# Two feed-forward blocks: the residual, the norm and the first gate/up tiles worked by halves of the tokens

## What is computed

```python
def rms_norm(x, g):
    xf = x.astype(jnp.float32)
    y = xf * lax.rsqrt(jnp.mean(xf * xf, axis=-1, keepdims=True) + RMS_EPS)
    return (y * g.astype(jnp.float32)).astype(x.dtype)

def conv_ffn(h, w_up, conv_w, conv_b, w_down):
    u = h @ w_up
    up = jnp.pad(u, ((0, 0), (CONV_W - 1, 0), (0, 0)))
    y = conv_b
    for j in range(CONV_W):
        y = y + up[:, j:j + S] * conv_w[j]
    gate, val = jnp.split(y, 2, axis=-1)
    return (jax.nn.silu(gate) * val) @ w_down
...
        x = x + g1 * mix
        h = rms_norm(x, norm_ffn[i]) * (1.0 + sc2) + sh2
        x = x + g2 * conv_ffn(h, ffn_w_up[i], ffn_conv_w[i], ffn_conv_b[i], ffn_w_down[i])
```

## Time and profile before

| | us |
|---|---|
| median of 3 runs | 1971.48 |
| lowest and highest | 1970.94, 1976.03 |
| profiled execution, its own time | 1970.52 |
| span from its first to its last instruction | 1968.7 |
| PE busy of the span | 1924.3 |

### The profile page before, as it was taken

The page is one execution under the profiler, slowest core; times in us unless marked ns, Lnnn a source line. Parts: engine busy times, 40 slices in busy tenths (PEclk is TensorE's granted clock), DMA queues, the critical chain, the costliest instruction groups (busy, mean ns, idle before and its releaser), DMA issues.

```text
span 1968.7 us, 26692 instructions
## 1 busy us (share of the span) xinstructions
PE 1924.3 (98%) x9254; PEld 1548.9 (79%) x9254; DVE 1084.2 (55%) x1657; ACT 562.4 (29%) x1119; POOL 1245.7 (63%) x729
## 2 busy tenths in 40 slices
PE   9999999999999899998999999999989999999999
PEld 7867788888888777777888888877766778888887
DVE  5966498877778325463443442144988543434412
ACT  4135300001124335661311121133457431111210
POOL 7642688887667565564766666645775357666664
PEclk9999999999999899999999999989999999999999
DMA  7520377766543222114332333213210023233331
GB/s 276 212 78 23 107 258 254 246 234 206 195 143 92 69 75 65 44 43 150 97 96 96 96 96 96 96 55 96 86 65 1 22 65 117 96 96 96 97 96 64
DMA packets 62326, 221.15 MB, mean 112 GB/s; under 512 B 6907, under 2 KB 7163, under 8 KB 62124
## 3 DMA queue, kind: packets, MB, share of 16 engines
q1 hardware_dynamic: 45216, 161.71, 25.7%
q10 hardware_dynamic: 17036, 58.46, 8.1%
HBM read 218.00 MB, written 2.14 MB: 112 GB/s over the span
## 4 chain that ended last, share of the span: by engine, by line
PE 92%; DVE 3%; POOL 2%; issue 2%; ACT 1%; DMA 0%; SPq 0%; POOLq 0%; DVEq 0%; ACTq 0%
PE bank L310 26%; PE bank L312 25%; PE bank L311 25%; PE bank L966 2%; PE bank L799 2%; PE bank L345 2%; PE bank L350 1%; PE bank L346 1%; PE bank L458 1%; PE bank L925 1%; PE bank L976 1%; PE bank L821 1%; POOL w_lo L1310 1%; PE bank L603 1%; PE bank L808 1%
## 5 line engine op out<-in xcount | busy, mean ns | idle before, releaser
L1310 POOL TENSOR_TENSOR w_lo<-raw,w_hi 128x1024 fp32r<-128x1024 f32 (+1 forms) x304 | 765.3, 2518 | 24.9
L310 PE MATMUL bank<-a_hi,w_hi 128*128 128x512 f32 x1960 | 764.7, 390 | 0.7 <-POOL w_lo L1310 0.4
L312 PE MATMUL bank<-a_hi,w_lo 128*128 128x512 f32 x1960 | 762.8, 389 | 0.0
L311 PE MATMUL bank<-a_lo,w_hi 128*128 128x512 f32 x1960 | 762.6, 389 | 0.0
L1305 POOL TENSOR_SCALAR w_hi<-raw 128x1024 fp32r<-128x1024 f32 x298 | 344.3, 1155 | 469.5 <-PE bank L312 360.4
L310 PEld LDWEIGHTS bank<-a_hi,w_hi 128*128 128x128 f32 x1960 | 367.9, 188 | 77.3 <-POOL w_lo L1310 0.8
L312 PEld LDWEIGHTS bank<-a_hi,w_lo 128*128 128x128 f32 x1960 | 367.9, 188 | 76.7
L311 PEld LDWEIGHTS bank<-a_lo,w_hi 128*128 128x128 f32 x1960 | 368.0, 188 | 76.1
L1904 DVE SCALAR_TENSOR_TENSOR tmp<-bank,vecs,tmp 128x511 f32<-128x511 f32 x88 | 65.9, 749 | 263.5 <-ACT tmp L1595 263.5
L1889 DVE CUSTOM_DVE_ANT_0 y<-y,cond 128x1024 f32<-128x1024 f32 x84 | 197.7, 2387 | 0.0
L1595 ACT ACTIVATE tmp<-bank,vecs 128x512 f32<-128x512 f32 x88 | 68.5, 781 | 372.7 <-PE bank L312 364.9
(11 more groups left out here) (295 smaller groups left out, 2250.5 us busy)
## 6 DMA issues: line engine op xcount, KB each, us to landing
raw<-in_stream SPq DMA_DIRECT2D x299, 512.0 KB, 3.5
y<-in_ada ACTq DMA_DIRECT2D x96, 512.0 KB, 4.6
x<-in_x SPq DMA_DIRECT2D x4, 512.0 KB, 6.5
bias<-in_bias ACTq DMA_DIRECT2D x1, 2048.0 KB, 14.8
y<-rel_rows ACTq DMA_DIRECT2D x1, 2048.0 KB, 8.1
bias<-rel_rows ACTq DMA_DIRECT2D x1, 2048.0 KB, 15.0
out<-x SPq DMA_DIRECT2D x8, 256.0 KB, 2.0
cond<-in_c ACTq DMA_DIRECT2D x1, 512.0 KB, 7.7
```

Source lines behind the costliest of these rows:

```text
L310: pe.matmul(o, lhs_hi, rhs_hi, start=start, stop=False, **kw)
L311: pe.matmul(o, lhs_hi, rhs_lo, start=False, stop=False, **kw)
L312: return pe.matmul(o, lhs_lo, rhs_hi, start=False, stop=stop, **kw)
L1310: m = pool.tensor_tensor(w_lo[:, s, part], raw[:, j, part], f32(w_hi[:, s, part]), ALU.subtract)
```

## The change

In both joints the last four output tiles and the first four gate/up tiles are worked in two halves of 256 tokens, h=0 and h=1.

- PE makes output tiles 0 to 3 as before, then tiles 4 to 7 for the tokens of h=0, then tiles 4 to 7 for those of h=1, with matmuls of 256 columns (`pe_late_halves`). Two tiles share a bank: tiles 4 and 5 of h=0 lie in bank 0, 6 and 7 in bank 1, those of h=1 in banks 2 and 3. The sum of squares of h=0 is taken after tile 4 of h=1, its spread after tile 5 of h=1.
- The gate/up tiles 0 to 3 follow in this order (`pe_early_halves`): tiles 0, 1 of h=0; the sum of squares of h=1; tiles 2, 3 of h=0 for five chunks; the spread of h=1; the last three chunks; then h=1 with all four tiles for chunks 0 and 1, tiles 0 and 1 for chunks 2 to 7, tiles 2 and 3 for chunks 2 to 7.
- `x`, the squares and their sum move in 12 pieces, 4 whole chunks and 2 x 4 halves; the running sum lies in `bank[7]` and no longer in SBUF. The scaled chunk lies in `bank[4]` or `bank[6]` (256 columns), no longer in `tmp`.
- DVE makes every low part, 16 halves. POOL makes none, and ACT's second copy goes. POOL's queue then holds only splits there.
- A block of output weights 4 to 7 is finished only with its tile of h=1, so POOL begins on gate/up blocks 0 to 3 at that point. `INVERSE_LAT` and `INVERSE_Q` only renumber counters of the inverse roots.

```diff
+HALVED = ("ffn0", "ffn1")
+HALF = S // 2
+HALF_PIECES = 4 + 2 * 4
+EARLY_SHARED = 2
...
+        def late_tile(c, h):
+
+            return bank[2 * h + (c - 4) // 2][:, HALF * (c % 2):HALF * (c % 2) + HALF]
...
+        def pe_late_halves(pe, name, norm):
+
+            for h in range(2):
+                for c in range(4, DC):
+                    s = (START[name] + c) % SPLIT
+                    if h == 0:
+                        pe.wait_ge(split_ready, START[name] + 1 + c)
+                    if c % 2 == 0:
+
+                        pe.wait_ge(x_ready, X_AT[name] + 2 * h + (c - 4) // 2 + 1)
+                    for k in range(DC):
+                        m = pe_three_passes(pe, late_tile(c, h), w_hi[:, s, k * P:(k + 1) * P], w_lo[:, s, k * P:(k + 1) * P],
+                                            a_hi[:, k, tokens_of(h)], a_lo[:, k, tokens_of(h)], k == 0, k == DC - 1, skip_group_check=True)
+                    m.then_inc(block_done if h else half_done, 1)
+                    if h and c == 4:
+                        pe_sum_half(pe, norm, 0)
+                    if h and c == 5:
+                        pe_spread_half(pe, norm, 0)
...
+            pe.wait_ge(split_ready, START[name] + 2)
+            products(0, (0, 1), range(DC))
+            pe_sum_half(pe, norm, 1)
+            pe.wait_ge(split_ready, START[name] + 4)
+
+            pe.wait_ge(x_ready, X_AT[update] + HALF_PIECES)
+            products(0, (2, 3), range(5))
+            pe_spread_half(pe, norm, 1)
+            products(0, (2, 3), range(5, DC))
+
+            products(1, range(4), range(EARLY_SHARED))
+            products(1, (0, 1), range(EARLY_SHARED, DC))
+            products(1, (2, 3), range(EARLY_SHARED, DC))
...
+            for c in range(DC):
+                scale(0, c)
+                if c:
+                    low(0, c - 1)
+                if c in (1, 2):
+                    add_piece(7 + c)
+                if c == 4:
+                    late_tiles(6, 1)
+                if c in (5, 6):
+                    add_piece(5 + c)
+            low(0, DC - 1)
+            inverse(1)
+            v.wait_ge(rstd_ready, NORM_INDEX[name] + 2)
+            for c in range(DC):
+                scale(1, c)
+                if c:
+                    low(1, c - 1)
+            low(1, DC - 1)
...
-            split_stream(START["out2"] + SPLIT + 2, START["gu2"] + AHEAD)
-            pool_lows("ffn0")
-            split_stream(START["gu2"] + AHEAD, START["qi"] + AHEAD)
+            split_stream(START["out2"] + SPLIT + 2, START["qi"] + AHEAD)
...
-            pe_tiles(pe, "out2", "battn", norm="ffn0")
-            pe_norm(pe, "ffn0", 1)
-            pe_tiles(pe, "gu2", "ffn0")
+            pe_tiles(pe, "out2", "battn", end=4)
+            pe_late_halves(pe, "out2", "ffn0")
+            pe_early_halves(pe, "gu2", "ffn0", "out2")
+            pe_tiles(pe, "gu2", done=4)
```

More of the change, by code:

```diff
@@ L354, in pe_tile_pair, with tokens_of, piece, pe_sum_half @@
                     after(k)
-        def pe_tiles(pe, name, split=None, norm=None):
-            n = COUNT[name]
+        def tokens_of(h):
+            return slice(HALF * h, HALF * h + HALF)
+        def piece(p):
+            if p < 4:
+                return p, slice(0, S)
+            return 4 + p % 4, tokens_of(p // 4 - 1)
+        def late_tile(c, h):
+            return bank[2 * h + (c - 4) // 2][:, HALF * (c % 2):HALF * (c % 2) + HALF]
+        def pe_sum_half(pe, name, h):
+            pe.wait_ge(sq_added, ADDED_AT[name] + (7, HALF_PIECES - 1)[h])
+            if h:
+                pe.wait_ge(scaled_ready, T_AT[name] + DC)
+            for t in (2 * h, 2 * h + 1):
+                m = pe.matmul(sum_columns(name)[:, t:t + 1], square_sum[:, GROUP_AT[name] % 2, t * P:(t + 1) * P], ones[:, 0:1],
+                              start=t == 2 * h, stop=True, skip_group_check=True)
+            m.then_inc(group_used, 1)
@@ new lines, in pe_early_halves, with products @@
+        def pe_early_halves(pe, name, norm, update):
+            pe_begin(pe, name)
+            pe.wait_ge(x_ready, X_AT[update] + 8)
+            def products(h, tiles, chunks):
+                sets = [(j, bank[j][:, tokens_of(h)], (START[name] + j) % SPLIT) for j in tiles]
+                for k in chunks:
+                    cols = slice(k * P, (k + 1) * P)
+                    pe.wait_ge(hi_ready, SPLIT_AT[norm] + DC * h + k + 1)
+                    for _, o, s in sets:
+                        pe.matmul(o, w_hi[:, s, cols], a_hi[:, k, tokens_of(h)], start=k == 0, stop=False, skip_group_check=True)
+                        pe.matmul(o, w_lo[:, s, cols], a_hi[:, k, tokens_of(h)], start=False, stop=False, skip_group_check=True)
+                    pe.wait_ge(lo_ready, LOW_AT[norm] + DC * h + k + 1)
+                    for _, o, s in sets:
+                        m = pe.matmul(o, w_hi[:, s, cols], a_lo[:, k, tokens_of(h)], start=False, stop=k == DC - 1, skip_group_check=True)
+                        if h and k == DC - 1:
+                            m.then_inc(block_done, 1)
+            pe.wait_ge(split_ready, START[name] + 2)
[9 more added lines that the diff above has]
+            products(1, (2, 3), range(EARLY_SHARED, DC))
@@ L360, in pe_tiles @@
+        def pe_tiles(pe, name, split=None, norm=None, done=0, end=None):
+            n = COUNT[name] if end is None else end
             follows = {"u": "z", "q": "u"}.get(name)
-            if not follows and name not in ("ki", "pe_gate"):
+            if not follows and name not in ("ki", "pe_gate") and not done:
                 pe_begin(pe, name)
-            done = 0
             if split == "attn":
@@ L445, in sum_columns @@
         def sum_columns(name):
+            if name in HALVED:
+                return rstd_bank[:, HALF:HALF + TT]
             return (bank[0] if name in ("post_ffn", "mix1") else bank[4])[:, 0:TT]
@@ L1559, in _ @@
                          lambda c: low_done("dattn", c), ready=((q_placed, 14), (q_placed_late, 2)))
-            pe_tiles(pe, "out3", "dattn", norm="ffn1")
-            pe_norm(pe, "ffn1", 1)
-            pe_tiles(pe, "gu3", "ffn1")
+            pe_tiles(pe, "out3", "dattn", end=4)
+            pe_late_halves(pe, "out3", "ffn1")
+            pe_early_halves(pe, "gu3", "ffn1", "out3")
+            pe_tiles(pe, "gu3", done=4)
             pe_down(pe, "down3", 2)
@@ L1918, in dve_conv, with dve_residual @@
             turn(FC // 2 - 1, split=True)
-        def dve_residual(v, update, layer, which, ready, n, norm=None):
-            slow = n == 4
+        def dve_residual(v, update, layer, which, ready, norm=None):
             for c in range(DC):
-                if norm and c and slow:
-                    dve_add_square(v, norm, c - 1)
                 ready(c)
-                v.scalar_tensor_tensor(x[:, c, :], bank[c % n][:], mod(layer, which, c), x[:, c, :], ALU.mult,
+                v.scalar_tensor_tensor(x[:, c, :], bank[c][:], mod(layer, which, c), x[:, c, :], ALU.mult,
                                        ALU.add).then_inc(x_ready, 1)
-                if norm and c and not slow:
+                if norm and c:
                     dve_add_square(v, norm, c - 1)
```

154 lines of the change are left out of this document (120 added, 34 removed).

## The result

The changed kernel takes 1959.07 us (median of 4 runs, 1957.28 to 1960.39) beside 1971.82 us for the kernel before on the same chip, 12.7 us less. The ratio of their runs is worked out apart and is not the quotient of the two medians: 0.9927 with a 95% interval of 0.9913 to 0.9942, which stands for 14.4 us less (11.4 to 17.2). Two later comparisons gave 0.9932 (0.9918 to 0.9946) and 0.9928 (0.9915 to 0.9942). The profiled execution took 1960.39 us, with a span of 1958.6 us.

What follows compares the result with a forecast made beforehand. PE, busy for 98% of the span, was taken as the bound. A stretch of 45.3 + 2.0 + 0.3 = 47.6 us, against 54.2 and 53.4, gains 12.4 us together, giving 1959.1 us; range 1955.5 to 1966.5.

Steps and rivals of the forecast that it cites:

- 384 half matmuls: Output tiles 4 to 7 and gate/up tiles 0 to 3 in halves: 45.3 us of PE time a stretch.
- four insertions: Two half sums and two half spreads between PE's matmuls in each stretch: 0.5 us each, together 2.0 us.
- waits: PE's waits for other engines in each block's stretch: nothing waits, but 0.3 us put in for thin slacks.
- The pitch: Time for a 256-column matmul on PE in the stretches: 0.118 us, with bounds 0.1133 and 0.120.
- The clock: PE at the joints: without long standstills the granted clock no longer falls; in block 2 the fall cost 2.5 us.
- The loss of the joint goes whole: Block 2's joint: PE's 7.11 us of only sums and transposes, 2.5 of fallen clock and 0.9 of sum all go.
- DVE keeps up: Block 2's stretch: DVE's 22 operations at some 0.45 us end at 934.4, 0.8 us before PE asks.
- The rival with 0.6 us: DVE becomes the bound in both stretches, at 0.6 us for an operation: 1967.5 us; chance 0.15.
- POOL keeps up: Gate/up tiles 2 and 3 of h=0: POOL's four splits, 3.53 us each, end 1.1 us before PE asks.
- The weight load: Rival: 188 ns weight loads no longer hidden under PE's 256-column matmuls, each stretch 26.9 us longer, 2013 us; chance 0.07.

Runs made afterwards that it cites:

- all-halved kernel: The kernel before, with gate/up tiles 4 to 43 of blocks 2 and 3 made of 256-column matmuls: 1997.34 us beside 1974.78, ratio 1.0125.
- the kernel with the norm behind the tiles: The changed kernel, with sum and spread of h=0 behind output tile 7 of h=1 in both blocks: 1969.62 us beside 1974.78, ratio 0.998.
- held up alone: The kernel before, with unread matmuls in PE's three waits at both joints: 1971.35 us beside 1974.78, ratio 0.9986.
- the experiment: The changed kernel, with six more 256-column DVE operations ahead of the first scaling of h=0 in blocks 2 and 3: ratio to the kernel before 0.9945.

## Why the prediction was right

Forecast 1959.1 us, measured 1959.07; forecast gain 12.4, stretches 12.97. That the two times agree to 0.03 us is luck: the changed kernel's own medians were 1959.07, 1960.21 and 1957.25. The closeness of the stretch, too, owes something to terms that cancel, so here they are one by one:

| term | predicted | measured |
|---|---|---|
| 384 half matmuls | 45.3 (0.118 each) | 46.1 (0.120) |
| four insertions | 2.0 | 1.3 |
| waits | 0.3 | 0.0 |
| sum | 47.6 | 47.35 |

- **The pitch** was mis-sized by 0.002 us. The full stream shows 0.120, the upper of the two figures taken from the earlier trace rows. But those rows don't hold it: starts printed to 0.01 us give a pair's half distance no closer than to 0.005, and the 32 pairs together lie at 0.118 as read. So the attention's matmuls, with one weight tile again and again, do start 0.002 us closer than these, and 0.120 as a bound came out by the rounding of one row. In the all-halved kernel the same weights twice in a row made no difference, so what makes the 0.002 us stays open.
- **The insertions** were put too high. A half sum was right (0.45 for 0.5). A half spread was put at 0.5 us, from the whole one's 1.11 us at the fallen clock, and took 0.21: a price read at 1.2 GHz doesn't hold where the clock stays up, and a row's length holds the draining too (the half spread's row is 0.38 us long here, with the next start 0.13 us behind its own).
- **The clock.** That it would not fall was right, PEclk 1.00 in both stretches. That its fall had cost 2.5 and 1.3 us was right for the kernel before as a part of a sum, and not as a price: held up alone it gave 1.24 and 0.47, since POOL's split of gate/up tile 2 stood 0.8 us behind it.
- **The loss of the joint goes whole**, 7.11 + 2.5 + 0.9: right, and shown by the kernel with the norm behind the tiles, which gives 5.7 of it back a joint.
- **DVE keeps up.** 22 operations were put at 0.45 us and an end at 934.4, 28.4 us into the stretch; the last low part of h=0 ended at 936.98, also 28.4 us in. Its slack, put at 0.8, is 0.8 by the trace and 0.55 by the experiment. The groups by line show why no operation was long:

```profile
L2105 DVE SCALAR_TENSOR_TENSOR a_lo<-bank,mods,a_hi 128x256 fp32r<-128x256 f32 x32 | 15.4, 480 | 1.2 <-ACT a_hi L1250 1.2
L2100 DVE SCALAR_TENSOR_TENSOR bank<-x,gains,bank 128x256 f32<-128x256 f32 x32 | 15.2, 485 | 6.1 <-PE bank L392 5.6
L2080 DVE SCALAR_TENSOR_TENSOR x<-bank,mods,x 128x256 f32<-128x256 f32 x16 | 7.0, 480 | 19.5 <-PE bank L322 19.5
L2077 DVE TENSOR_TENSOR bank<-bank,squares 128x256 f32<-128x256 f32 x12 | 5.1, 428 | 0.6
```

  0.48 us as put, from the row of another line. The rival with 0.6 us did not come. The rule that speaks against small tiles (the Trainium skill, VectorE: DVE Perf Modes, "The TRN2 errata — SBUF-src ops pay a fixed extra latency per instruction") holds in its cost: 480 ns for 256 columns against the 750 of the earlier trace rows for 512 leaves 210 ns that don't shrink, and DVE's busy time rose by 4 us though its additions of squares got cheaper. The page speaks of operations that read SBUF, and what makes the fixed part in these, which read PSUM too, no run shows. It does not decide, because DVE stays 0.5 us short of being the bound.
- **POOL keeps up.** Slack 1.1 put, 1.0 read and 1.0 measured. A split was 3.5 us each time. The longer operations of the earlier trace rows, 1.49 us at 902.71 and 2.82 at 907.79, stood beside DVE's additions of squares from two SBUF operands in the kernel before (902.23 to 903.29 and 907.67 to 908.36), and the changed kernel has none of these in its stretches.
- **The weight load** stays hidden at 0.120 us, over 3840 matmuls with new weights. The estimate from the Trainium skill (TensorE: Matmul & The Clock Gate, "LDWEIGHTS (loading the stationary operand)") of 107 ns fits under it. Its 109 ns between starts ("Back-to-back issue gap") is not reached: 0.120 us here.

What the runs did not test: whether the two insertions of h=1 could stand elsewhere, a smaller set of halved tiles, and two parts of the change by themselves, the low parts taken off POOL and the running sum moved to PSUM.

## What to carry to other kernels

Where a reduction over all of an operand's rows stands between two streams of matmuls, cut the free dimension (here the tokens) on both sides of it, so that one half's chain runs under the other half's tiles. It costs the narrower matmul's extra (here 0.0067 us each, 2.6 us a joint) and pays the whole wait (10 us), as long as every slack of the engines beside it is counted and kept, down to the order in which tiles free the weight buffers. And price a fallen clock by what stands second in the queue, not by its own length.
